# Seventeen sums over partitions as products of a rounded part and its rest, a packed unit for the rotary keys, and another order of best_eight

## The reference

```python
def rmsnorm(x, g):
    xf = x.astype(jnp.float32)
    y = xf * lax.rsqrt(jnp.mean(xf * xf, axis=-1, keepdims=True) + EPS) * g.astype(jnp.float32)
    return y.astype(x.dtype)

# retention: mean, then variance, over the 512 values of a head
mu = jnp.mean(of, axis=-1, keepdims=True)
var = jnp.mean(jnp.square(of - mu), axis=-1, keepdims=True)

# MLA
kv_a = rmsnorm_2(h, norm_kv_g) @ w_kv_a
c_kv = rmsnorm_2(kv_a[..., :MLA_KV_RANK], kv_a_norm_g)
k_rope = apply_rope(kv_a[..., MLA_KV_RANK:][:, :, None, :], cos, sin)
```

## Time and profile before

| | |
|---|---|
| median of 3 runs | 1382.91 us (1382.76 to 1383.61) |
| the profiled execution, its own time | 1382.96 us |
| its span in the trace | 1381.2 us |
| TensorE busy | 1369.9 us, 99% |
| VectorE busy | 998.6 us, 72% |
| ScalarE busy | 701.7 us, 51% |
| GpSimd busy | 271.2 us, 20% |
| instructions | 24679 |

### The profile page before, as it was taken

One profiled execution on the slowest core, in us unless ns is written; L12 is line 12 of the kernel. 1 busy time (PEld: TensorE's weight loads), 2 busy tenths in 40 slices (PEclk: granted clock), 3 DMA queues, 4 the chain that ended last, 5 costly groups with the idle time before them and its releaser, 6 DMA issues.

```text
span 1381.2 us, 24679 instructions
## 1 busy us (share of the span) xinstructions
PE 1369.9 (99%) x9900; PEld 1303.0 (94%) x9900; DVE 998.6 (72%) x1576; ACT 701.7 (51%) x1154; POOL 271.2 (20%) x266
## 2 busy tenths in 40 slices
PE   9999999999989999999999999999999999999998
PEld 9999999999989888889999999999999999988886
DVE  6688666656796988788666775766657786798843
ACT  7465544444746555544334564544444465655543
POOL 0026000022143000032244544000022523120000
PEclk9999999999999999999999999999999999999999
DMA  8334565665443655555444355555554554465552
GB/s 273 123 122 153 188 184 183 190 185 165 136 138 108 221 171 195 178 168 193 151 141 142 123 182 155 183 183 171 165 183 131 177 145 150 133 221 183 188 193 76
DMA packets 220313, 229.72 MB, mean 166 GB/s; under 512 B 13648, under 2 KB 207432, under 8 KB 220200
## 3 DMA queue, kind: packets, MB, share of 16 engines
q1 hardware_dynamic: 219088, 226.24, 51.3%
q10 hardware_dynamic: 1112, 1.90, 0.6%
HBM read 226.80 MB, written 1.33 MB: 165 GB/s over the span
## 4 chain that ended last, share of the span: by engine, by line
PE 97%; DVE 1%; DMA 1%; POOL 0%; ACT 0%; SPq 0%; issue 0%; POOLq 0%
PE ps L556 27%; PE ps L554 20%; PE ps L555 20%; PE ps L551 14%; PE ps L1057 1%; PE ps L1056 1%; PE ps L1055 1%; PE ps L924 1%; PE ps L614 1%; PE ps L616 1%; PE ps L615 1%; PE ps L847 1%; PE ps L638 1%; PE ps L731 1%; PE ps L914 1%; DMA raw<-in_gla_w_in 1%
## 5 line engine op out<-in xcount | busy, mean ns | idle before, releaser
L1105 ACT ACTIVATE uh<-raw 128x1024 fp32r<-128x1024 f32 (+4 forms) x452 | 446.2, 997 | 457.1 <-PE ps L556 392.8
L1663 DVE TENSOR_TENSOR ul<-raw,uh 128x1024 fp32r<-128x1024 f32 (+3 forms) x449 | 529.1, 1185 | 152.0 <-PE ps L556 93.3
L556 PE MATMUL ps<-xx,ul 128*128 128x272 f32 (+1 forms) x2136 | 611.1, 286 | 0.0
L554 PE MATMUL ps<-xx,uh 128*128 128x272 f32 (+1 forms) x1448 | 427.0, 295 | 0.8 <-ACT h L1231 0.8
L555 PE MATMUL ps<-xx,uh 128*128 128x272 f32 (+1 forms) x1448 | 415.9, 287 | 0.0
L556 PEld LDWEIGHTS ps<-xx,ul 128*128 128x128 f32 x2136 | 402.1, 188 | 0.0
L554 PEld LDWEIGHTS ps<-xx,uh 128*128 128x128 f32 x1448 | 272.9, 188 | 5.3 <-issue 1.7
L555 PEld LDWEIGHTS ps<-xx,uh 128*128 128x128 f32 x1448 | 273.3, 189 | 1.1
L556 PE MATMUL ps<-aa,ul 128*128 128x272 f32 (+1 forms) x928 | 265.1, 286 | 0.0
L551 PE MATMUL ps<-xx,uh 128*128 128x512 f32 x704 | 247.4, 395 | 0.0
L554 PE MATMUL ps<-aa,uh 128*128 128x272 f32 (+1 forms) x796 | 231.4, 291 | 0.0
(11 more groups left out here) (313 smaller groups left out, 1573.4 us busy)
## 6 DMA issues: line engine op xcount, KB each, us to landing
raw<-in_ffn_w SPq DMA_DIRECT2D x62, 1024.0 KB, 5.3
raw<-in_ffn_w_in SPq DMA_DIRECT2D x44, 1024.0 KB, 5.2
raw<-in_ret_w_in SPq DMA_DIRECT2D x24, 1024.0 KB, 5.2
raw<-in_ffn_w_out SPq DMA_DIRECT2D x16, 1024.0 KB, 5.5
raw<-in_gla_w_in SPq DMA_DIRECT2D x11, 1024.0 KB, 5.1
raw<-in_ret_w_o SPq DMA_DIRECT2D x8, 1024.0 KB, 5.2
raw<-in_dsa_w_in SPq DMA_DIRECT2D x7, 1024.0 KB, 5.2
raw<-in_ffn_w_out SPq DMA_DIRECT2D x8, 768.0 KB, 4.9
```

The source lines that it names most:

```text
L554: e.matmul(ps[:, 0:n1 - n0], hi[:, k, :], x.hi[:, k0 + j, n0:n1], start=first and j == 0, stop=False)
L556: i = e.matmul(ps[:, 0:n1 - n0], lo[:, k, :], x.hi[:, k0 + j, n0:n1], start=False, stop=last and j == len(ks) - 1)
L1105: i = e.activation(unit_hi(u)[:, :, cols], a, ACT.Copy)
L1663: i = e.tensor_tensor(unit_lo(u)[:, :, cols], a, unit_hi(u)[:, :, cols].bitcast(F32), ALU.subtract)
```

## The change

1. **Seventeen sums.** A rounded tile of ones, `ones_r`, is made once by GpSimd. For 17 of the 22 calls of `total` GpSimd makes two more instructions behind the sum (`parted`): the rounded sum into a free slot of `ah`, and the sum minus it into the same slot of `al`. TensorE then does two f32r products (`total_of_parts`) instead of one f32 product. The 17 are `gt` of c = 0, 1, 2, `n1`, `n2`, `n5`, `n6`, `rm` and `rr` of the four heads, `mct`, `mqt`. The counts of the semaphores go up by two in each. `gt` of c = 3, `n3`, `n4` with its companion, `n7` and `dct` stay.
2. `squares` waits for another product before it starts for n1 and n5, the last that read the shared slot.
3. **The rotary keys' unit** is packed: no pads, its rest goes into columns 64 to 127 of `uh`, 16 products instead of 24. VectorE copies the upper half of the result out of PSUM and adds the lower half, and the four rotations read this from SBUF.
4. **best_eight.** The rounds 0 to 3 stand together, ahead of two weight rests, where there was a rest, two rounds, a rest, two rounds.

```diff
+        ones_r = sb("ones_r", [P, P], F32R)
-            slabs.append(([(view, W[:, 512:576].rearrange("(k p) n -> p k n", p=P))], [(view, "pad")]))
+            slabs.append(([(view, W[:, 512:576].rearrange("(k p) n -> p k n", p=P))], [(view, "packed")]))
-        PACKED = 0
+        PACKED = {0: slice(32, 48), [u for u in range(NU) if units[u][2] == "packed"][0]: slice(64, P)}
...
+            def total_of_parts(key, s_sum, v, j, n):
+
+                ps = small(key, "A")
+                w.wait_ge(s_const, 5)
+                w.wait_ge(s_sum, v)
+                e.matmul(ps[:, 0:n], ones_r[:, :], ah[:, j, 0:n], start=True, stop=False)
+                done(e.matmul(ps[:, 0:n], ones_r[:, :], al[:, j, 0:n], start=False, stop=True), key)
...
-                    together([(f, "g", 0), (f, "g", 1)], x, n0, T, lambda: squared(13))
+                    together([(f, "g", 0), (f, "g", 1)], x, n0, T,
+                             lambda: total_of_parts(("n", 2 * f + 1), s_ssq[2 * f + 1], 15, 20, T - n0))
...
-                total(("gt", c), "A", s_gsq, 3 * c + 3, ssq[1 + c % 2], T)
+                if c < 3:
+                    total_of_parts(("gt", c), s_gsq, 5 * c + 5, 20 + c % 2, T)
+                else:
+                    total(("gt", c), "A", s_gsq, 18, ssq[2], T)
...
-                        total(("rm", hd), "A", s_rsum, 3 * hd + 3, ssq[1], T)
+                        total_of_parts(("rm", hd), s_rsum, 5 * hd + 5, 20, T)
...
             index_head(6)
             index_head(7)
-            lo()
             for b in range(2):
                 w.wait_ge(s_acc, 15 + b)
                 e.memset(d_acc[0:64, HIDDEN[b]], OUT_OF_REACH).then_inc(s_best, 1)
-            best_eight(0)
-            best_eight(1)
+            for k in range(4):
+                best_eight(k)
             lo()
-            best_eight(2)
-            best_eight(3)
+            lo()
...
-            ps = lin.bank("mkr")
+
+            ps, keys = lin.bank("mkr"), tmp[4]
+            e.tensor_copy(keys[0:64, :], ps[64:P, 0:T]).then_inc(s_mcs, 1)
+            w.wait_ge(s_mcs, 3)
+            e.tensor_tensor(keys[0:64, :], keys[0:64, :], ps[0:64, 0:T], ALU.add).then_inc(lin.empties("mkr", "D"), 1)
+            w.wait_ge(*lin.emptied("mkr"))
             low, high = slice(0, 32), slice(32, 64)
-            e.tensor_tensor(tmp[0][low, :], ps[low, 0:T], m_cs[low, :], ALU.mult)
+            e.tensor_tensor(tmp[0][low, :], keys[low, :], m_cs[low, :], ALU.mult)
...
+            def parted(total, n, j, s_sum, v):
+
+                w.wait_ge(s_sum, v)
+                e.tensor_scalar(ah[:, j, 0:n], total, 1.0, None, ALU.mult).then_inc(s_sum, 1)
+                w.wait_ge(s_sum, v + 1)
+                e.tensor_tensor(al[:, j, 0:n], total, ah[:, j, 0:n].bitcast(F32), ALU.subtract).then_inc(s_sum, 1)
...
-                w.wait_ge(*aux.full(("n", i - 1)))
+                w.wait_ge(*aux.full({1: ("gt", 2), 5: ("rm", 3)}.get(i, ("n", i - 1))))
...
+                if i != 4:
+                    parted(total, T - n0, 20, s_ssq[i], 13)
...
+            w.wait_ge(s_const, 4)
+            e.tensor_scalar(ones_r[:, :], ones[:, :], 1.0, None, ALU.mult).then_inc(s_const, 1)
...
             squares(6, 2, 0)
-            pad(PADS[2])
...
             low_rank_squares(ssq[1][:, :], m_ck, "mc", range(4), s_ckss, T)
-            w.wait_ge(s_ckss, 7)
+            parted(ssq[1][:, :], T, 21, s_ckss, 7)
             low_rank_squares(ssq[2][:, 0:TQ], m_cq, "ma", range(6), s_cqss, TQ)
+            parted(ssq[2][:, 0:TQ], TQ, 19, s_cqss, 11)
```

More of the change, by code:

```diff
@@ L140, in build @@
         tmp = [tmps[:, i, :] for i in range(6)]
-        NAR = 13760
+        NAR = 13632
         arena = sb("arena", [P, NAR])
@@ L423, in unit_n @@
             kc = units[u][2]
-            return 8 if kc == "pad" else 6 if kc == "heads" else kc
+            return 8 if kc in ("pad", "packed") else 6 if kc == "heads" else kc
         def unit_hi(u):
@@ L438, in pieces @@
             src = view(raw[s % NRAW])
-            if kc == "pad":
+            if kc in ("pad", "packed"):
                 return [(src, slice(0, src.shape[2]))]
@@ L849, in attended @@
                 done(i, key)
-            together(["dki", ("dc", 0)], x, 0, T, lambda: total(("n", 2), "A", s_ssq[2], 13, ssq[0], T))
+            together(["dki", ("dc", 0)], x, 0, T, lambda: total_of_parts(("n", 2), s_ssq[2], 15, 20, T))
             chunk(("dc", 1), "D", x, 0, T)
@@ L940, in ret_after @@
                     if r == 7:
-                        total(("rm", hd), "A", s_rsum, 3 * hd + 3, ssq[1], T)
+                        total_of_parts(("rm", hd), s_rsum, 5 * hd + 5, 20, T)
                 hd -= 1
                 if 0 <= hd < 4 and r == 3:
-                    total(("rr", hd), "A", s_rsq, 7 * hd + 7, ssq[2], T)
+                    total_of_parts(("rr", hd), s_rsq, 9 * hd + 9, 21, T)
             def both_totals():
@@ L992, in mla_logits @@
                 done(i, ("mL", hd))
-            together([("ma", 0), ("ma", 1)], x, NM, T, lambda: total(("n", 6), "A", s_ssq[6], 13, ssq[0], T))
+            together([("ma", 0), ("ma", 1)], x, NM, T, lambda: total_of_parts(("n", 6), s_ssq[6], 15, 20, T))
             for c in range(4):
@@ L1000, in _ @@
                 if c == 3:
-                    total("mct", "A", s_ckss, 7, ssq[1], T)
+                    total_of_parts("mct", s_ckss, 9, 21, T)
             for hd in range(8):
@@ L1007, in _ @@
                 if hd == 3:
-                    total("mqt", "A", s_cqss, 11, ssq[2], TQ)
+                    total_of_parts("mqt", s_cqss, 13, 19, TQ)
             chunk(("mr", 0, 0), "D", x_cq, NM, T)
@@ L2245, in _ @@
             w.wait_ge(s_mcs, 2)
-            ps = lin.bank("mkr")
-            low, high = slice(0, 32), slice(32, 64)
-            e.tensor_tensor(tmp[0][low, :], ps[low, 0:T], m_cs[low, :], ALU.mult)
[L2249 to L2252, removed]
+            ps, keys = lin.bank("mkr"), tmp[4]
[3 more added lines that the diff above has]
+            w.wait_ge(*lin.emptied("mkr"))
+            low, high = slice(0, 32), slice(32, 64)
+            e.tensor_tensor(tmp[0][low, :], keys[low, :], m_cs[low, :], ALU.mult)
+            e.tensor_tensor(tmp[1][low, :], keys[high, :], m_sn[high, :], ALU.mult)
+            e.tensor_tensor(tmp[2][low, :], keys[low, :], m_sn[low, :], ALU.mult)
+            e.tensor_tensor(tmp[3][low, :], keys[high, :], m_cs[high, :], ALU.mult).then_inc(s_mcs, 1)
+            w.wait_ge(s_mcs, 4)
             w.wait_ge(s_mzero, 1)
@@ L2431, in _ @@
                     e.tensor_tensor(sq if v else total, o, o, ALU.mult).then_inc(s_gsq, 1)
-                w.wait_ge(s_gsq, 3 * c + 2)
+                w.wait_ge(s_gsq, 5 * c + 2)
                 e.tensor_tensor(total, total, sq, ALU.add).then_inc(s_gsq, 1)
+                if c < 3:
+                    parted(total, T, 20 + c % 2, s_gsq, 5 * c + 3)
                 if c == 3:
@@ L2490, in ret_sum @@
                     w.wait_ge(*aux.emptied(("rO", 4 * hd + v)))
-                    w.wait_ge(s_rsum, 3 * hd + v - 1)
+                    w.wait_ge(s_rsum, 5 * hd + v - 1)
                     e.tensor_tensor(total, total, o[v], ALU.add).then_inc(s_rsum, 1)
+                parted(total, T, 20, s_rsum, 5 * hd + 3)
             def ret_squares(hd):
@@ L2502, in ret_squares @@
                     if v:
-                        w.wait_ge(s_rsq, 7 * hd + 2 * v)
+                        w.wait_ge(s_rsq, 9 * hd + 2 * v)
                         e.tensor_tensor(total, total, sq, ALU.add).then_inc(s_rsq, 1)
+                parted(total, T, 21, s_rsq, 9 * hd + 7)
             def ret_y_lo(c):
```

12 lines of the change are left out of this document (6 added, 6 removed).

## The result

The changed kernel takes 1387.25 us (median of 8 runs, 1385.05 to 1387.79) against 1382.95 us before on the same chip: 1.0026 times as long, 95% interval 1.0017 to 1.0035. It is 4.3 us slower where 2.6 faster was forecast, and it lies outside the range.

The account below looks back on a forecast made before the run. TensorE, busy 99% of the span, was taken to bound the kernel. Ten sums -2.1, six sums +2.2, best_eight -2.4, rotary keys +0.2 and first parts -0.5 gave -2.6: 1380.4 us, range 1376.8 to 1383.6.

Parts of the forecast that it names:

- Ten covered sums, -2.1: Three GLA sums, `rm` and `rr` of the first three heads, `mqt`: parts ready in time, each saves 0.21 us.
- best_eight, -2.4: Start of the sparse attention: all four rounds before VectorE's wait for ScalarE bring the mask's chain 2.4 us earlier.
- Four norms, 2.0 of waiting: `n1`, `n2`, `n5`, `n6`: second part 2.6 us after the sum, late by 0.65 (n1, n6) and 0.35 (n2, n5).
- Nobody else suffers: Head 3: VectorE waits there for TensorE or ScalarE, and a late total moves TensorE and what follows together.
- rm 3 and rr 3, late by 0.6 and 0.9: Head 3's two sums: parts and later squares outlast covers of 2.0 and 2.03 us; 1.5 us of waiting together.
- The bound from above at `n1`, 3.3: Norm sum `n1`: longest time from sum to end of second part, with weight rests in the way; 2.6 was taken.
- Rotary keys, +0.2: MLA rotary keys: 1.2 us off TensorE, less 0.8 waiting for `x_ck` and 0.6 contention; between -0.4 and +0.8.
- -0.5 for faster first parts: Six places with little cover: first parts may be faster with a constant than with a pointer, -0.5 us.
- The third: Rival: a row of VectorE instructions shuts GpSimd out at `n6`, head 3, `n1` and the rotation; 1385.5 us, chance 0.08.
- The first: Rival: the cover holds and the six waits shrink to about 0.1 us each; 1377.4 us, chance 0.27.
- The second: Rival: VectorE's chains give less, rotation 1.2 us later or half of best_eight's 2.4 lost; 1381.6 us, chance 0.2.
- The line that I wrote for being wrong: The six sums with little cover: the sum is wrong if TensorE waits at none, or over 2 us at one.

Follow-up runs that it names:

- e1: The kernel before with only the four best_eight searches moved ahead of two weight rests: 1380.39 us, 0.9979 of the kernel before.
- e6: The changed kernel with GpSimd's squares of head 3 moved ahead of its three rests of y: 1382.78 us, 0.9996 of the kernel before.
- e10: The changed kernel with the sum behind head 3's mean (`rm` 3) as one full product again: 1382.93 us, 0.9997 of the kernel before.
- e2: The kernel before with only the rotary keys' unit packed: 1384.32 us, 1.0009 of the kernel before.
- e7: The changed kernel with the sums `n6` and `mct` as full products again, rotary keys still packed: 1383.66 us, 0.9999 of the kernel before.
- e5: The changed kernel with TensorE making overwritten products of ones during the waits for `rr` 3 and `x_ck`: 1383.88 us, 1.0006 of the kernel before.
- e4: The changed kernel with `rm` 3, `rr` 3, `n6` and `mct` as full products and the rotary keys unpacked: 1378.70 us, 0.9967 of the kernel before.
- e3: The kernel before with only the seventeen sums as products of parts: 1387.02 us, 1.0024 of the kernel before.
- e9: The changed kernel with head 3's squares ahead of three rests of y and VectorE's last four rotary instructions behind the rests of `x_ck`: 1380.32 us, 0.9978.
- e8: e4 with the packed rotary keys back and VectorE's last four rotary instructions moved behind the rests of `x_ck`: 1377.70 us, 0.9959 of the kernel before.

## Why the prediction was wrong, step by step

**Ten covered sums, -2.1**: right. They save about 0.2 us each in the trace, none of them waits.

**best_eight, -2.4**: right. -2.5 in the changed kernel, -3.0 alone (e1), where TensorE's wait behind the mask falls to 1.5; the waits behind L2079 are gone as forecast.

**Four norms, 2.0 of waiting**: too high. 0.3, 0.1, 0.1, 0.4 = 0.9. At `n6` both parts ran at 0.95 and 1.14 beside VectorE, so the whole weight rest that I put between them wasn't paid there. But it was paid on the other side: VectorE's rows beside them grew by 0.2 and 0.5. I had asked who else suffers only at head 3 ("Nobody else suffers") and put nothing on VectorE's side at `n6`. That is one of the failed steps; the 0.7 us went, with 0.3 of lateness already there, into the raw buffer's release, the transfer of the q_a weights, and `x_ck`.

**rm 3 and rr 3, late by 0.6 and 0.9**: the mechanism was right, the sizes were wrong: 1.0 and 2.6. At `rr` 3 I took the delay of the squares (0.3 of it net) and 2.6 from the sum to the end of the second part. My own terms gave more: squares 1.3 later and TensorE 0.6 later are 0.7 net, and with the 0.6 from the parts 1.3 instead of 0.9. Measured are 785.23 - 781.77 = 3.5 us from the product of `rm` 3 to the first square, 0.5 more than before (788.08 - 785.12 = 3.0), and 3.7 for the parts, 1.1 more than taken. The bound from above at `n1`, 3.3, was the better guess for both parts in a stretch where a weight rest comes every 2.5 us (787.44, 789.96, 792.48). e6 and e10 show that squares 1.4 to 1.9 us earlier decide between 2.3 and 3.7.

The Trainium skill, SBUF — State Buffer, section Who interferes with whom, has a GpSimd instruction that reads SBUF and a VectorE instruction with two SBUF inputs exclude each other for a whole instruction. This trace agrees: the first part, with one input only, takes 1.74 us in all three places where it is issued inside a weight rest of 1024 columns, 1.17 inside one of 512, and 0.89 to 0.97 in the other thirteen. The mean of 964 ns that I read in the earlier trace rows came from places where nothing was in its way, and I carried it to places where something was.

**Rotary keys, +0.2**: near as far as it went. 0.8 of waiting and 0.6 of contention make 1.4; e2 and e7 show 1.7, and e2 costs 1.0 as a whole instead of 0.2 (its `mct` is whole, so 0.2 of saving isn't in it). That VectorE would start 1.0 earlier was too much: the earlier trace rows show it idle for 0.76 there, and in e2 it starts 0.9 earlier (1078.26). What failed is the frame: I weighed this chain by itself, and the sums in another part of the change delay the same chain, through a transfer. Two edits that each eat into one cover have to be added before the cover is taken off.

**The clock, not in the sum at all**: the largest failed step, 3.0 us. I priced every wait at its own length. The trace of before had one long wait, 2.4 us, with no fall of the clock, and I had not asked what a longer or another one would do. e5 shows that the stretches come from the idle time in the waits.

**-0.5 for faster first parts**: not there. They took 0.94 to 0.97 at the four norms, as the row that I read, and 1.74 at head 3.

Put together: 1380.4, +1.9 for `x_ck`, +2.1 for head 3, +3.0 for the clock, +0.5 for the first parts, -1.1 for the norms: 1386.8, against 1387.25 measured. Of the rest 0.3 is what TensorE lost at 1087 us.

**The rivals.** The third came nearest in time (1385.5) but not in its mechanism: TensorE's waits before sums come to 3.4 us, not over 6, and no GpSimd part was shut out by the row of eight at `n6`. The first held for the thirteen sums of e4 alone. The second named the right chain, late by 1.2 more than in the main case; it was 1.9 more, and 3.4 with the clock. The line that I wrote for being wrong, one of the six waits over 2 us, is the one that came true.

## What to carry to other kernels

A wait of TensorE isn't worth its length alone: look at the granted clock in the microseconds behind it, in the kernel with the change, since the kernel before may not show it. Where several edits take from the slack of one chain, add their delays first; a queue of transfers and a shared port carry a delay to places that no edit touches. And work handed to a helper engine pays where its result has slack: here ten of seventeen places gained 0.2 us each, three norms came out even, and the other four with the rotary unit cost more than everything else brought.

## What the runs showed of the hardware

TensorE was granted half its clock for about 3.4 us in seven stretches of these traces (two in the changed kernel, one each in e3, e6, e7, e9 and e10), each around the end of a wait: from 0.1 us before TensorE took up work again (e10, at 1089.30 us, the first product at 1089.43) to 1.3 us after it. The waits ahead were 2.4 (`rr` 3), 3.1, and once 1.8 us. None followed 1.7 us (e2, e7), 1.2 us (e3), the 1.5 us behind the mask, or the 2.4 us behind the mask in the traces of the kernel before, e2 and e3:

```profile
388.25 0.97 PE L815 MATMUL ps<-arena 128*128 128x144 f32 x4 [0.58 <-DVE arena L2079]
...
394.45 0.30 PE L832 MATMUL ps<-cst,arena 128*128 128x128 f32 x1 [2.40 <-DVE arena L2057]
```

So the length of the wait alone doesn't decide, and what else does wasn't tested.

One trace speaks for one run. The mean granted clock, which is on record for every run, says more. In the traces without such a stretch it is 0.999 or 1.000 (only the end of the span, where TensorE has nothing left to do, lies at half clock, for 0.1 to 2.8 us), and one stretch takes 0.001 off. All 32 runs of e1, e4, e5 and e8, where TensorE is never idle for more than 1.5 us behind the first products, have 0.999 or 1.000. In the changed kernel six runs have 0.997 (1387.1 to 1387.8 us) and two 0.998 (1385.1 and 1385.2). And the kernel before, beside the experiments, has 0.998 in 29 of 75 runs, at 1383.5 us in the mean against 1382.9 for the twelve with 1.000. So it too probably has a stretch of half clock in some of its runs, which its one trace doesn't show; where, no trace says, and its long wait is the one behind the mask. The kernels with a stretch in their trace also scatter more: 2.2 to 3.7 us between the fastest and the slowest run, against 0.5 to 1.5 us in e1, e2, e4, e5 and e8. That fits a stretch that comes in some runs and not in others.

A transfer changed its landing time: the last of `in_mla_w_q_a` took 5.45 us from issue to ScalarE's first use before (1070.31 to 1075.76) and 6.65 in the changed kernel (1071.37 to 1078.02). Over all traces it is 5.4 to 5.5 us in the six without `n6`'s parts and 6.3 to 6.65 in five of the six with them; e5, the sixth, has 5.5, and its chain to `x_ck` is only 0.4 us shorter for it. What the transfer met on the queues wasn't looked into.
